# Two transformer blocks on one core: the operands of the feed-forward matmuls moved to addresses that are multiples of 2048 bytes

## What is computed

```
for layer in 0, 1:                                   # first block
    h = hybrid_mixer(x)                              # convolution, differential attention, delta rule
    x = layer_norm(ALPHA * x + h)
    f = swiglu(x)            if layer == 0           # width 2816
    f = moe_swiglu(x)        if layer == 1           # 8 experts of width 3584, two for each token
    x = layer_norm(ALPHA * x + f)
x = x + attention_and_lru(rms_norm(x)) @ w_out       # second block
x = x + (gelu(gate) * val) @ w_down                  # gate, val = conv3(rms_norm(x) @ w_up), width 3072
out = rms_norm(x)

swiglu(x) = (silu(x @ w1) * (x @ w3)) @ w2
```

## The kernel before

| tensor | address | past a multiple of 2048 | past a multiple of 64 |
|---|---|---|---|
| `b_X` | 36800 | 1984 | 0 |
| `b_XT` | 44992 | 1984 | 0 |
| `b_ring0` (the others 16384 on) | 61376 | 1984 | 0 |
| `b_arena` and `e_xh` | 132064 | 992 | 32 |
| `e_xl`, `e_th`, `e_tl`, `e_yh`, `e_yl` | | 992 | 32 |
| `e_hi0` (and all of `e_hi`, `e_lo`) | 175200 | 1120 | 32 |

## Time and profile before

### The profile page before, as it was taken

One profiled execution on the slowest core, in us unless ns is written; L12 is line 12 of the kernel. 1 busy time (PEld: TensorE's weight loads), 2 busy tenths in 40 slices (PEclk: granted clock), 3 DMA queues, 4 the chain that ended last, 5 costly groups with the idle time before them and its releaser, 6 DMA issues.

```text
span 2347.3 us, 26804 instructions
## 1 busy us (share of the span) xinstructions
PE 2185.0 (93%) x10612; PEld 1739.6 (74%) x10612; DVE 1396.5 (59%) x1775; ACT 1114.6 (47%) x1117; POOL 1188.1 (51%) x473
## 2 busy tenths in 40 slices
PE   8999899989997899999999999999899996888997
PEld 7577588775775677777778777888678774747997
DVE  4564643355656677767677775333377776455665
ACT  1232333312321676767676674333376672534544
POOL 0120154301200798989898894554399891202553
PEclk9999999989998999999999999999999998979999
DMA  8101454522014699989899895554499893314560
GB/s 303 70 1 44 169 200 144 197 96 72 1 36 163 236 359 324 358 301 360 321 352 356 304 355 211 179 179 179 145 331 355 318 359 134 107 36 174 203 211 24
DMA packets 208095, 484.95 MB, mean 207 GB/s; under 512 B 9168, under 2 KB 13008, under 8 KB 206928
## 3 DMA queue, kind: packets, MB, share of 16 engines
q1 hardware_dynamic: 207952, 483.02, 56.9%
HBM read 481.96 MB, written 1.05 MB: 206 GB/s over the span
## 4 chain that ended last, share of the span: by engine, by line
PE 86%; DVE 8%; ACT 2%; issue 2%; POOL 1%; DMA 1%; DVEq 0%; ACTq 0%; SPq 0%; POOLq 0%
PE bank L947 21%; PE bank L949 20%; PE bank L948 20%; PE bank L584 10%; PE bank L776 5%; PE bank L591 3%; DVE b_arena L1323 1%; PE bank L737 1%; DVE b_X L1323 1%; ACT e_hi L2166 1%; POOL b_arena L2630 1%; DVE b_arena L1329 1%; PE bank L854 1%; PE bank L693 1%; PE bank L1216 1%
## 5 line engine op out<-in xcount | busy, mean ns | idle before, releaser
L2723 POOL TENSOR_TENSOR e_lo<-b_ring,e_hi 128x512 fp32r<-128x512 f32 (+1 forms) x401 | 1123.4, 2823 | 656.1 <-ACT e_hi L2166 656.0
L1795 DVE TENSOR_TENSOR e_lo<-b_ring,e_hi 128x1536 fp32r<-128x1536 f32 (+2 forms) x407 | 775.1, 1905 | 492.8 <-ACT e_hi L2166 491.5
L2166 ACT ACTIVATE e_hi<-b_ring 128x2048 fp32r<-128x2048 f32 (+1 forms) x407 | 774.5, 1906 | 348.1 <-PE bank L949 341.7
L947 PE MATMUL bank<-e_hi,e_xh 128*128 128x512 f32 (+1 forms) x1200 | 481.8, 401 | 28.8 <-POOL e_lo L2723 9.4
L948 PE MATMUL bank<-e_lo,e_xh 128*128 128x512 f32 (+1 forms) x1200 | 472.8, 394 | 0.0
L949 PE MATMUL bank<-e_hi,e_xl 128*128 128x512 f32 (+1 forms) x1200 | 472.7, 394 | 0.0
L947 PEld LDWEIGHTS bank<-e_hi,e_xh 128*128 128x128 f32 x1200 | 227.6, 190 | 98.8 <-issue 47.5
L947 PE MATMUL bank<-e_hi,e_th 128*128 128x512 f32 x688 | 273.3, 397 | 0.0
L949 PE MATMUL bank<-e_hi,e_tl 128*128 128x512 f32 x688 | 271.7, 395 | 0.0
L948 PE MATMUL bank<-e_lo,e_th 128*128 128x512 f32 x688 | 271.4, 395 | 0.0
L949 PEld LDWEIGHTS bank<-e_hi,e_xl 128*128 128x128 f32 x1200 | 227.7, 190 | 52.6
(11 more groups left out here) (233 smaller groups left out, 2346.7 us busy)
## 6 DMA issues: line engine op xcount, KB each, us to landing
b_ring<-in_moe_w SPq DMA_DIRECT2D x168, 2048.0 KB, 8.2
b_ring<-in_w_in SPq DMA_DIRECT2D x15, 2048.0 KB, 9.2
b_ring<-in_ffn_w SPq DMA_DIRECT2D x15, 2048.0 KB, 7.9
b_ring<-in_w_up SPq DMA_DIRECT2D x12, 2048.0 KB, 7.9
b_ring<-in_w_down SPq DMA_DIRECT2D x6, 2048.0 KB, 8.8
b_ring<-in_w_o SPq DMA_DIRECT2D x4, 2048.0 KB, 7.7
b_gain<-in_gains SPq DMA_DIRECT2D x7, 1024.0 KB, 4.7
b_ring<-in_w_out SPq DMA_DIRECT2D x2, 2048.0 KB, 8.3
```

What stands on the lines that cost most here:

```text
L947: e.matmul(out, ah, bh, start=first, stop=False)
L1795: e.tensor_tensor(lo[:, 0:at], raw[:, 0:at], r32(hi[:, 0:at]), ALU.subtract).then_inc(lo_dve.sem)
L2166: return e.activation(out, x, ACT.Copy)
L2723: e.tensor_tensor(lo[:, at:], raw[:, at:], r32(hi[:, at:]), ALU.subtract).then_inc(lo_pool.sem)
```

## The change

Two tensors that nothing reads or writes are laid down: `pad`, 264 float32 ahead of the arena, and `gap`, 480 float32 ahead of the split buffers.

```diff
         rank, flag = sb("rank", [128, 2, 8]), sb("flag", [128, 8], mybir.dt.int32)
+        sb("pad", [128, 264])
         with nc.sbuf_tensor("b_arena", [128, 23808], F32) as arena:
             pass
         with ExitStack() as over:
...
             e_gate = [[eb(f"gate{i}", [128, 8]) for i in range(3)], [eb("gateb", [128, 8])]]
+            eb("gap", [128, 480])
             split = [[eb(f"{n}{i}", [128, 2048], F32R) for n in ("hi", "lo")] for i in range(NH)]
```

## The result

The changed kernel takes 2333.6 us (median of four, 2329.96 to 2336.45) against 2350.25 us before (median of four, 2348.8 to 2352.02): a ratio of 0.9928, 95% interval 0.9911 to 0.9945, some 17 us faster. The forecast was no change, 2351.5 us, and the range from 2340 to 2380 doesn't hold it. In a second comparison it came to 2333.69 against 2352.29 us, 0.9919 (0.9905 to 0.9932). The profiled execution, the fastest of the four, took 2329.96 us, its span 2328.0.

The account below looks back on a forecast made before the run. It took TensorE, busy 2185.0 of 2347.3 us, mostly with the matmuls of `three()`, as the bound. All terms summed to 0, so it predicted from the median of the runs: 2351.5 us, range 2340 to 2380.

Parts of the forecast that it names:

- Moving and stationary operands of the feed-forwards: Feed-forward matmuls, 5568 of 512 columns and 1248 of 256: cost or gain of each taken as 0.
- (b): Layer 0's narrow group: slices crossing a 2048-byte boundary cost nothing to be seen, at most 3 ns a matmul.
- (d): Mixers' float32 matmuls: 429.4 ns per 512-column record, no surplus, same time from ring and arena places.
- Reading (a): Feed-forward matmuls: the surplus over the clock's pace grows with columns, 0.447 ns a column plus some 4 ns fixed.
- Reading (c): Same matmuls at granted clock 0.5: 425 ns, surplus gone, so supply tops out near a column every 0.445 ns.
- Rival B: Feed-forward matmuls: the surplus comes from the position within 64 bytes and goes; 101.5 us faster, 2250 us; chance 0.20.
- Rival C: Feed-forward matmuls: stationary and moving operands collide at one position, 4 ns each, 27 us slower, 2379 us; chance 0.14.
- The other steps: Reservations, the engines' split writes and the mixers' tensors at new addresses: each taken as 0 us.
- the mixers' tensors: Mixers' tensors in the arena move by 1056 bytes, from 992 to 0 past 2048: no effect, 0 us.
- The test named for B and C: Start-to-start time of twelve 512-column matmuls: 2.56 us if unchanged, 2.36 if the surplus goes, over 2.60 if operands collide.

Follow-up runs that it names:

- moving_only: Only gap, 232 float32, so only the split pieces moved to multiples of 2048, against the kernel before: 2353.24 us against 2351.07, ratio 1.0011.
- the table: Separate kernel without the two blocks, only float32r matmuls at pairs of (moving, stationary) byte places past a multiple of 2048; (32, 32): 226.7 ns for 512 columns.
- stationary_only: Pad 264 and gap 248 float32, so tokens and turned rows moved but split pieces stayed, against the kernel before: 2353.15 us, ratio 1.0012.
- by_64: Only pad, 8 float32, moving everything in the arena by 32 bytes to multiples of 64, against the kernel before: 2351.6 us, ratio 1.0003.

## Why the prediction was wrong

**The step that failed** is "Moving and stationary operands of the feed-forwards": I took 0 between bounds of -18.0 and +4 ns. Measured: -5.8 ns where the row is undisturbed, -3.5 in narrow experts, and +1.3 for the 256-column matmuls. I chose 0 because (b) and (d) were the nearest rows in which an address differs. Both were read rightly and both stand: crossing costs nothing (`moving_only`, and (32, 32) in the table), and float32 is blind to the place. But (b) moves one operand by multiples of 256 bytes and (d) has no float32r matmul, and no row of before that I read varied the distance of the two at full pace: it was 128 modulo 256 in all 5568 matmuls of `three()` with 512 columns. The trace of before had one other group, which the prediction didn't read: the rows go back to the tokens (L1062, L1063) with `e_yh` or `e_yl` moving and `e_PT` stationary, both 224 past a multiple of 256, so at distance 0. They come in rows of eight, too short to settle; behind the first interval the mean is 230.8 ns before and 230.3 after, so they hint at another pace and couldn't have given the 226.7. I noted that no row showed the other position within 64 bytes and didn't ask which other properties had never varied.

**Reading (a)** took the pace as a line, 0.447 ns a column and 4 ns fixed, from two widths. They were two patterns. At distance 0 the line is 0.417 ns a column and 13.3 ns fixed for 256, 384 and 512 columns (448 has 16.0). The inference to a supply that tops out at 0.445 ns a column was wrong: from 256 to 512 columns the time grows at the clock's pace.

**Reading (c)** holds (425 ns at 1.2 GHz; the median interval at the granted clock 0.5 is 427 ns before and after, and in `moving_only` and `stationary_only` too, so at four distances), and its use, that the address isn't needed to explain the surplus, was a comfort and no test.

**Rival B** had the sign and not the property: the place within 64 bytes does nothing (`by_64`). Its price of 101.5 us supposed that the whole surplus goes; a third of it went, and the four narrow experts between gathers take 128.0 to 130.0 us, above the 122.6 at which it had the DMA engines stop the gain; even so waits took back about half of the gain there. A part of this rival, for an effect of one operand alone or of the fixed 4 ns, was given 2300 to 2345 us, and 2333.6 lies in it. That is luck: one operand alone gains nothing (`moving_only`, `stationary_only`), and the fixed part grew from 4 to 13.3 ns.

**Rival C** had the property with the wrong sign. It named the distance of the two operands, saw that the change brings both to one place, and priced that as a collision. For 256 columns the sign is right (+1.3 ns, where it had 4); its sign of longer loads isn't there (median 188 ns, as before); for 512, where the time is, equal places are the best there are.

**The other steps held.** ScalarE, VectorE and GpSimd kept their times (busy within 0.4%), and the mixers' tensors brought nothing (`stationary_only`). The test named for B and C, twelve starts in 2.36 or over 2.60 us, and 2.56 for the forecast, missed between them: 11 x 226.7 gives 2.49.

**What stays open** is the cause in the hardware. The pace depends on the distance modulo 256 bytes, at full clock and not at half, in float32r and not in float32 (no other type was run), and for some distances has two patterns that the start selects. A conflict of the load's and the stream's reads would depend on a distance, and the spread between distances does shrink with 64 stationary columns; but at D = 0 a shorter load is slower, which speaks against the simple form. None of these runs looks inside the memory.

## What to carry to other kernels

Where matmuls of one kind fill the time, work out the pace from their starts and compare it with columns over clock; if something is left over, shift one operand by a few tens of bytes against the other before anything else is rebuilt. Here 128 bytes of padding were worth 0.85% and alignment itself nothing, and the best shift differs by the width of the matmul. When a trace shows a resource at one setting only, an effect of that setting can't be argued away from it: list what never varied and give it a chance, or measure a table with nothing else on the core. And before a few us of one profile are put down to a change, compare how long the granted clock was low in both: here that was 1.3 to 3 us a stage.

## What the runs showed of the hardware that was not expected

- float32r matmuls with their own weight loads: 226.7 to 237.3 ns for 512 columns, 4.7% between the best and the worst distance of the operands' starts. 0, 256, 512 and 1024 have the same pace, and so have 64 and 1088.
- A distance of 4 bytes (one element) is the worst that was tried, 237.3 ns; 8 has 233.3 and 16 has 231.6.
- The intervals are periodic, not noisy: all equal at distance 0 (227, 226, 227 in whole ns, 226.7), a cycle of seven from 228 to 241 at 128, 229 and 238 in turn as the second pattern of 128. At distance 0 it takes 4 to 11 matmuls to settle after an interruption, at 232 ns on average in the row shown, so frequent short waits cost beyond their own length.
- float32 matmuls (429.2 ns a record of 512 columns) show none of it.
